# Moving two thirds of one layer's conditioning product from TensorE to row sums on VectorE

## What is computed

```python
for l in range(2):
    mod  = silu(c)     @ w_ada[l] + b_ada[l]      # 6 x 1024 numbers, for x
    cmod = silu(c_ctx) @ w_ada[l] + b_ada[l]      # 6 x 1024 numbers, for xc
    shift1, scale1, gate1, shift2, scale2, gate2 = split(mod, 6)
    y, yc = mixer(x * (1 + scale1) + shift1, xc * (1 + cscale1) + cshift1)   # GLA, MLA and conv branch
    x = layer_norm(ALPHA * x + gate1 * y)
    x = layer_norm(ALPHA * x + gate2 * conv_ffn(x * (1 + scale2) + shift2))
    # the same for xc with cmod, in layer 0 only
```

## Time and profile before

| | us |
|---|---|
| median of 3 runs | 2666.77 (2665.58 to 2667.77) |
| the profiled execution | 2666.24 |
| its span | 2664.2 |
| PE busy | 2612.0, 98% |
| DVE busy | 1852.5, 70% |
| ACT busy | 827.1, 31% |
| GpSimd (POOL) busy | 87.1, 3% |

### The profile page before, as it was taken

How to read it: one execution, slowest core, us unless ns; L and a number is a source line. 1 busy time by engine, 2 the same in 40 slices (tenths; PEclk the granted TensorE clock), 3 DMA queues, 4 the chain that set the end, 5 groups by cost and what they waited for, 6 DMA issues and landing times.

```text
span 2664.2 us, 43805 instructions
## 1 busy us (share of the span) xinstructions
PE 2612.0 (98%) x17212; PEld 2213.2 (83%) x17212; DVE 1852.5 (70%) x3779; ACT 827.1 (31%) x1856; POOL 87.1 (3%) x115
## 2 busy tenths in 40 slices
PE   9999899999999999999999999999999999999998
PEld 8777799979676887567887888888799987898998
DVE  7882299644787377788857766644467568768997
ACT  2033144132554112553232423200445222133431
POOL 0000000000231000000000000000012000000000
PEclk9999999999999999999999999999999999999999
DMA  5553544432332221221222222222321431243443
GB/s 209 183 191 119 215 159 160 178 126 85 118 140 88 80 95 72 87 95 72 81 94 95 95 79 95 80 95 95 116 73 58 149 135 64 95 150 136 163 171 127
DMA packets 86922, 314.21 MB, mean 118 GB/s; under 512 B 9488, under 2 KB 11536, under 8 KB 86464
## 3 DMA queue, kind: packets, MB, share of 16 engines
q1 hardware_dynamic: 85216, 304.78, 32.1%
q0 software_dynamic: 1504, 6.64, 0.7%
HBM read 310.33 MB, written 1.05 MB: 117 GB/s over the span
## 4 chain that ended last, share of the span: by engine, by line
PE 68%; DVE 3%; ACT 1%; issue 1%; DMA 0%; DVEq 0%; ACTq 0%; SPq 0%
PE ps L621 39%; PE ps L924 14%; PE ps L730 2%; PE ps L3460 1%; PE ps L3377 1%; PE ps L3378 1%; PE ps L3325 1%; PE ps L937 1%; PE ps L3429 1%; PE ps L962 1%; PE ps L1815 1%; PE ps L2130 1%; PE ps L2294 1%; PE ps L2248 0%; PE ps L2271 0%
## 5 line engine op out<-in xcount | busy, mean ns | idle before, releaser
L621 PE MATMUL ps<-sb 128*128 128x128 f32 (+1 forms) x8344 | 1353.7, 325 | 7.2 <-ACT sb L697 3.3
L621 PEld LDWEIGHTS ps<-sb 128*128 128x128 f32 x8344 | 1244.7, 191 | 118.2 <-issue 8.5
L924 PE MATMUL ps<-sb 128*128 128x256 f32 (+1 forms) x2320 | 612.3, 421 | 8.8 <-DVE sb L1003 3.7
L924 PEld LDWEIGHTS ps<-sb 128*128 128x128 f32 x2320 | 439.0, 190 | 167.8 <-issue 101.3
L3638 DVE SCALAR_TENSOR_TENSOR sb<-sb 128x512 f32<-128x512 f32 (+1 forms) x480 | 275.5, 615 | 8.7
L793 ACT COPY sb<-ps 128x256 f32<-128x256 f32 (+1 forms) x221 | 76.4, 346 | 406.0 <-PE ps L621 342.5
L634 DVE TENSOR_TENSOR sb<-sb 128x512 f32<-128x512 f32 x160 | 109.7, 686 | 128.0 <-PE ps L621 90.9
L697 ACT COPY sb<-ps 128x128 f32<-128x128 f32 (+1 forms) x252 | 75.3, 299 | 217.9 <-PE ps L621 211.7
L811 DVE TENSOR_TENSOR sb<-sb,ps 128x256 f32<-128x256 f32 (+1 forms) x118 | 45.5, 386 | 103.0 <-PE ps L621 73.1
L636 DVE TENSOR_TENSOR sb<-sb 128x512 f32<-128x512 f32 x160 | 110.6, 692 | 5.5
L4282 DVE SCALAR_TENSOR_TENSOR sb<-sb 128x512 f32<-128x512 f32 (+1 forms) x176 | 101.0, 615 | 14.6 <-ACT sb L4228 9.6
(11 more groups left out here) (533 smaller groups left out, 2749.7 us busy)
## 6 DMA issues: line engine op xcount, KB each, us to landing
sb<-in_w SPq DMA_DIRECT2D x575, 512.0 KB, 3.7
sb<-in_two POOLq DMA_DIRECT2D x2, 1088.0 KB, 7.3
sb<-in_x SPq DMA_DIRECT2D x2, 512.0 KB, 4.8
sb<-in_ctx POOLq DMA_DIRECT2D x1, 1024.0 KB, 7.8
sb<-in_v_bias POOLq DMA_DIRECT2D x2, 512.0 KB, 3.6
sb<-in_par SPq DMA_DIRECT2D x1, 764.0 KB, 6.6
sb<-in_s5b POOLq DMA_DIRECT2D x1, 512.0 KB, 7.8
sb<-in_s5c POOLq DMA_DIRECT2D x1, 512.0 KB, 9.8
```

The costliest lines, as they stand in the source:

```text
L621: ins = pe.matmul(o, w, xs(i), start=(fresh and i == 0), stop=(i == len(ws) - 1), skip_group_check=True)
L924: ins = pe.matmul(o[:, i * n:(i + 1) * n], w, rhs(k), start=(k == 0), stop=(k == kt - 1))
```

## The change

Layer 1's groups 0 to 7 (blocks a = 0 to 31) are taken from PE. Groups 8 to 11 stay, at the places that are left: two before the first GLA unit, one in head 3, one in the closing of the layer norm. The 32 blocks come from a transposed copy of the weights, `wa`: 32 tiles of 128 outputs x 1024 inputs, 512 KB each. `crow` holds c and c_ctx, each repeated on 128 partitions (512 KB each). ACT applies silu to `crow` in place. DVE multiplies a tile by a silu'd row and sums along it in one scalar_tensor_tensor with `accum_out`. Blocks 16 to 31 are wanted for x alone (one such instruction each) and are computed in `v_gla_in(0)`; blocks 0 to 15 are wanted for x and context (two each) and are computed in the down projection of layer 0's FFN. So 48 instructions of 128x1024 are added. `wa` and `crow` come by GpSimd's queue into 3 buffers in the first place and 4 in the second; a buffer is filled again when DVE is done with the block in it. The coefficients of layer 1's first modulation (`v_coef(1, 0)`) and two scalings move from the start of `v_ln_close` to the end of the last turn of the down projection.

```diff
-ADA_HEADS = (1, 3, 5)
+ADA_HEADS = (3,)
+ADA_COLUMNS = list(range(16, 32)) + list(range(16))
+ADA_EARLY = 16
+ADA_BY_PE = [list(range(6 * D // 512)), list(range(8, 6 * D // 512))]
+ROW_BUFS = (3, 4)
...
-        ADA_FILL = {"start": 2, 1: 1, 2: 1, 3: 1, 4: 1, 5: 1, 6: 1}
+        ADA_FILL = {"start": 2}
...
+        def p_columns(e):
+
+            first = e * ADA_EARLY
+            for i in range(first, ADA_EARLY if e == 0 else len(ADA_COLUMNS)):
+                _, b, _ = column_buf(i)
+                if i - first >= ROW_BUFS[e]:
+                    po.wait_ge(vector_steps, at(("column", i - ROW_BUFS[e])))
+                po.dma_start(column_bufs[e][:, b, :], t_in["wa"][i]).then_inc(column_loaded[b], 16)
+
+        def p_cond_rows(e):
+            for c in range(1 + e):
+                po.dma_start(cond_rows[e][:, c, :], t_in["crow"][c]).then_inc(loaded["crow%d" % e], 16)
+
+        def a_cond_rows(e):
+            act.wait_ge(loaded["crow%d" % e], at("loaded_crow%d" % e))
+            for c in range(1 + e):
+                act.activation(cond_rows[e][:, c, :], cond_rows[e][:, c, :], ACT.Silu).then_inc(scalar_steps, A.step(("crow", e)))
...
+        def v_columns(n):
+            for i in range(column_next[0], column_next[0] + n):
+                e, b, turn = column_buf(i)
+                a, w = ADA_COLUMNS[i], column_bufs[e][:, b, :]
+                ve.wait_ge(scalar_steps, at(("crow", e)))
+                ve.wait_ge(column_loaded[b], 16 * (turn + 1))
+                if e:
+                    if i > ADA_EARLY:
+                        ve.wait_ge(vector_steps, at(("product", i - 1)))
+                    ve.scalar_tensor_tensor(out=product_out, in0=w, scalar=1.0, in1=cond_rows[e][:, 1, :], op0=ALU.mult, op1=ALU.mult,
+                                            accum_out=mod[:, 1, a, 1:2]).then_inc(vector_steps, V.step(("product", i)))
+                    ve.wait_ge(vector_steps, at(("product", i)))
+                ve.scalar_tensor_tensor(out=w, in0=w, scalar=1.0, in1=cond_rows[e][:, 0, :], op0=ALU.mult, op1=ALU.mult,
+                                        accum_out=mod[:, 1, a, 0:1]).then_inc(vector_steps, V.step(("column", i)))
+            column_next[0] += n
...
@@ a_gla_in, behind the two reads of k
+            if l == 0:
+                a_cond_rows(0)
             key, b = ("kp", l, 2), [pc(("b_in", l, "k"), m) for m in (2, 3)]
@@ v_gla_in
             v_pair_parts(g, ("kp", l, 2), lambda m, c: kT[:, 2 + m, c * TX:(c + 1) * TX])
+            if l == 0:
+                v_columns(3)
...
                     pair_sums(g, i)
+                    v_columns(3)
                     key = ("qp", l, m)
...
                 pair_sums(g, i + 1 + j)
+                if l == 0:
+                    v_columns((1, 2, 2, 2)[j])
+                    if j == 3:
+                        v_columns_bias(16, 32, 1)
@@ v_down_parts, turn p
+            by_columns = f.tag == ("f2", 0)
+            if by_columns and p in (1, 2):
+                v_columns(2)
             for q in (3 * p + 2, 3 * p + 3):
                 if q < 12:
                     down_sums(f, q)
+                if by_columns and q == 3 * p + 2:
+                    v_columns(3)
+            if by_columns and p == 3:
+                v_columns_bias(0, 16, 2)
+                f.columns_done()
@@ a_r
+            if (l, m) == (0, 0):
+                act.wait_ge(vector_steps, at(("column", ADA_EARLY - 1)))
@@ gpsimd
                 po.dma_start(two, t_in["two"]).then_inc(loaded["two%d" % l], 16)
                 if l == 0:
+                    p_cond_rows(0)
+                    p_columns(0)
                     for u, unit_ in enumerate(units(l)):
                         p_gla_prod(l, u, *unit_)
...
                 p_pads(l)
+                if l == 0:
+                    po.wait_ge(vector_steps, at(("u2", 0, FT - 1)))
+                    p_cond_rows(1)
+                    p_columns(1)
```

More of the change, by code:

```diff
@@ L264, in build @@
         slab_loaded = [sem(f"slab_loaded{i}") for i in range(RING)]
-        loaded = {n: sem("loaded_" + n) for n in ("x0", "x1", "par", "one", "rows1", "s5", "two0", "two1", "rowsl0", "rowsl1", "cond", "ctx")}
+        loaded = {n: sem("loaded_" + n) for n in ("x0", "x1", "par", "one", "rows1", "s5", "two0", "two1", "rowsl0", "rowsl1", "cond", "ctx", "crow0", "crow1")}
+        column_loaded = [sem(f"column_loaded{i}") for i in range(4)]
         out_stored = sem("out_stored")
@@ L1809, in t_ada @@
                 pe.wait_ge(scalar_steps, at("cond"))
-            o = open_job(("ada", l), hold=True) if j == 0 else ps[:, job_of[("ada", l)], :]
+            first = j == ADA_BY_PE[l][0]
+            o = open_job(("ada", l), hold=True) if first else ps[:, job_of[("ada", l)], :]
             c0 = 2 * (ADA - 1 - j)
@@ L1814, in t_ada @@
                 q = 32 * (k % 4)
-                ins = pe.matmul(o[q:q + 32, :], cond[:, k, c0:c0 + 32], w, start=(j == 0 and k < 4), stop=(j == ADA - 1 and k >= 4),
+                ins = pe.matmul(o[q:q + 32, :], cond[:, k, c0:c0 + 32], w, start=(first and k < 4), stop=(j == ADA - 1 and k >= 4),
                                 skip_group_check=True)
@@ L1822, in more_ada @@
             for _ in range(n):
-                t_ada(ada_done[0] // ADA, ada_done[0] % ADA)
+                l, j = [(l, j) for l in range(LAYERS) for j in ADA_BY_PE[l]][ada_done[0]]
+                t_ada(l, j)
                 ada_done[0] += 1
@@ L1847, in v_ada_tr, with column_buf @@
                                  ALU.add).then_inc(vector_steps, V.step(("free", ("adt", l))))
             ve.wait_ge(vector_steps, V.n)
-            for part in range(2):
+            for part in range(l, 2):
                 a0 = (3 * part + 1) * DT
                 ve.tensor_scalar(mod[:, l, a0:a0 + DT, :], mod[:, l, a0:a0 + DT, :], 1.0, None, ALU.add).then_inc(vector_steps, V.step(("mod", l)))
+        def column_buf(i):
+            e = int(i >= ADA_EARLY)
+            q = i - e * ADA_EARLY
+            b = q % ROW_BUFS[e]
+            return e, b, q // ROW_BUFS[e] + (len(range(b, ADA_EARLY, ROW_BUFS[0])) if e and b < ROW_BUFS[0] else 0)
@@ L3920, in v_coef @@
         def v_coef(l, part, gain, beta):
+            w = 1 if (l, part) == (1, 1) else 2
             a = coef[:, 2 * l + part]
[L3923 to L3926, removed]
+            up = mod[:, l, (3 * part + 1) * DT:(3 * part + 2) * DT, 0:w]
+            by = lambda key: pc(key, 0, DT).unsqueeze(2).to_broadcast([P, DT, w])
             ve.wait_ge(vector_steps, V.n)
-            ve.tensor_tensor(a[:, DT:2 * DT, :], a[:, DT:2 * DT, :], mod[:, l, 3 * part * DT:(3 * part + 1) * DT, :], ALU.add).then_inc(vector_steps, V.step(("coef", l, part)))
+            ve.tensor_tensor(a[:, 0:DT, 0:w], up, by(gain), ALU.mult).then_inc(vector_steps, V.step())
+            ve.tensor_tensor(a[:, DT:2 * DT, 0:w], up, by(beta), ALU.mult).then_inc(vector_steps, V.step())
+            ve.wait_ge(vector_steps, V.n)
+            ve.tensor_tensor(a[:, DT:2 * DT, 0:w], a[:, DT:2 * DT, 0:w], mod[:, l, 3 * part * DT:(3 * part + 1) * DT, 0:w], ALU.add).then_inc(vector_steps, V.step(("coef", l, part)))
         def part_of(gate):
@@ L3939, in v_ln_close, with next_coef @@
                 v_turns(mix_src[l])
-            if nxt is not None:
+            def next_coef():
                 v_coef(*nxt, gain, beta)
@@ L4292, in build @@
         for n_, s_ in loaded.items():
[L4293 removed]
+            known_val = {"s5": 32, "rowsl0": 32, "rowsl1": 32, "cond": 16, "crow1": 32}.get(n_, 16)
             table["loaded_" + n_] = (n_, known_val)
@@ L4596, in _layout @@
     return m
-_SHAPES = dict(x=(P, DT, TX), ctx=(P, DT, TX), cond=(P, CONDW * DT), one=(P, len(ONE_NAMES), P), two=(P, TWO_COLS), par=(P, len(PARAMS)),
+_SHAPES = dict(wa=(len(ADA_COLUMNS), P, D), crow=(2, P, D), x=(P, DT, TX), ctx=(P, DT, TX), cond=(P, CONDW * DT), one=(P, len(ONE_NAMES), P), two=(P, TWO_COLS), par=(P, len(PARAMS)),
                rows1=(P, ROWS_1), s5b=(P, 2 * S5_TILES * 32), s5c=(P, 2 * S5_TILES * 32), rowsl=(LAYERS, P, 512), v_bias=(LAYERS, P, 1024))
```

29 lines of the change are left out of this document (25 added, 4 removed).

## The result

The changed kernel takes 2654.52 us (median of 4 runs, 2651.56 to 2655.41) against 2667.27 (4 runs, 2665.58 to 2670.03): ratio 0.9949, 95% interval 0.9932 to 0.9966. The direction and most of the mechanism held; the size did not.

The account below looks back on a forecast made before the run. PE was taken as the bound, busy 2612.0 of 2664.2 us. Removed groups -12.1 and ACT's delay +3.7, with sums and queues at nothing, gave -8.4 on the median 2666.77: 2658.4 us, range 2654 to 2664.

Parts of the forecast that it names:

- What is removed: Eight 1.92 us groups off PE in GLA units 1 to 6 and MLA heads 1 and 5: 12.1 us gained.
- What ACT gets: Start of input projections: table load and silu delay ACT's copy of P1; PE idles 2.0 us, 3.7 with clock loss.
- The clock term: Behind PE's 2.0 us idle stretch in the input projections, 3.3 us at half clock lose 1.7 us.
- the row lands early or the clock stays: Rival, input projections: cost 0.4 in place of 3.7 us, 2655.1 us; clock alone kept, 2656.7; chance 0.18.
- DVE's sums: 48 sums of 1.23 us in input projections and down projection, hidden in DVE's waits: cost nothing.
- the first early place: Start of the input projections: DVE was said to wait about 4.5 us for PE, covering three sums of 3.7 us.
- The rival of half rate: Accumulating sums take 2.46 us; some 2 us reach the path at the last late place: 2660.4 us, chance 0.10.
- The slower rival: Columns' round trip, refill 8.7 us, leaves DVE standing and PE stalling in the projections: 2674 us, chance 0.08.
- the last place: Tightest late place, end of the down projection: six sums end by 1856.7, P1 read at 1859.45, hidden by 2.7 us.

Follow-up runs that it names:

- e11: Changed kernel with each late column's context sum made three times (32 more sums in the down projection): 2680.04 us, ratio to before 1.0043.
- e10: Changed kernel with each early column summed twice (16 more sums on DVE): 2653.99 us, ratio to before 0.9955.
- e13: Changed kernel with three columns (1.5 MB) issued by GpSimd ahead of the conditioning row: 2662.81 us, ratio to before 0.9982.
- e6: Changed kernel with the silu behind the copies of P1 and head 3's group moved to GLA unit 2: 2653.04 us, ratio to before 0.9946.
- e2: Changed kernel with the first column (512 KB) issued by GpSimd ahead of the conditioning row: 2655.39 us, ratio to before 0.9960.
- e4: Changed kernel without the added sums, rows and columns, groups still removed (the table's second column; result not the reference's): 2654.14 us, ratio to before 0.9953.
- e9: Changed kernel with two buffers in place of three for the early columns: 2655.84 us, ratio to before 0.9956.

## Why the prediction missed in size

- **What is removed**, forecast 12.1, measured 13.1 (neither). Place by place, from the second column of the table: start and unit 1 2.46 (forecast 1.92), unit 2 and unit 3 together 2.07 (0 + 1.92), unit 4 2.05, unit 5 2.06 (1.92 each), unit 6 0.81 (0.6), the heads 3.83 (3.84), with 0.17 given back between. Which units give and which don't was read rightly from the earlier trace rows. The surplus of the first place is not the group's: before, the clock is at half behind the wait of 1.27 us for weights there, and in the other trace it isn't, though its wait is 0.6 longer.
- **What ACT gets** is the step that failed: 2.0 us of waiting and 1.7 of clock, where the changed kernel shows a wait of 0.50 and full clock. The first goes back to "it lands 8.7 us later, 560.85" for `two`. In the changed kernel the DMA rows of the same stretch (us from issue to landing at the end) are

```profile
sb<-in_two POOLq DMA_DIRECT2D x1, 1088.0 KB, 7.5
...
sb<-in_crow POOLq DMA_DIRECT2D x1, 512.0 KB, 8.2
```

  GpSimd issues them at 554.81 and 555.33: landings at 562.3 and 563.5, the row 1.2 behind `two`, against my 1.4 for its 512 KB. That part held. But `two` took 7.5 us, and in the fourteen traces, in which its issue and all ahead of it are the same, it took 6.3 to 8.7, 7.9 in the middle. The 8.7 of the earlier trace rows is the longest of them. One execution's transfer time was used as if it were the kernel's. PE's wait follows it, in the kernels that leave the row and the silu where they are: 0.30 us with 6.3 and 7.1 (there the table load ends last), 0.50 with 7.5, about 0.95 with 7.9, 1.27 with 8.2. Carried on to 8.7 that is an estimated 1.7, near my 2.0. I did give bounds, 0.4 to 4.3, but put the value at a row that has no spread beside it.
- **The clock term**, 1.7 us, was added to the unhappy value and is not borne out even for it: a wait of 2.58 us at the same place, made on purpose, was followed by full clock in its one trace. Together the two terms were forecast at 3.7 us and measured at 0.75 in the projections and 0.57 in the end. That is 3.1 of the miss, the removed work the other 1.0; -8.4 less both is -12.5, what the changed kernel's trace shows. That is the rival "the row lands early or the clock stays", -11.7 us, to which I gave 0.18: by its two costs, though not by its reason, for the row did not pass `two`.
- **DVE's sums** were priced rightly (1.22) and hidden in all 13 places; PE waits for DVE in none of them. One reading was off without harm: the 4.5 us of the first early place is a wait for a weight's DMA (4.56 in the timeline), not for PE. The Trainium skill's rule that I weighed, half rate for a scalar_tensor_tensor with two SBUF sources that aren't bf16 ("Vector Engine (DVE) Microarchitecture Reference", "Points that are easy to get wrong"), doesn't show here with an accumulator either: 128x1024 fp32 in 1.22 us.
- **The rival of half rate** had a wrong price, 2 us. e11, which adds as many late sums and by their dependence a little more time, cost 21.7; 32 times 1.15 alone is 36.8 against 23.4 left, 13 us without any loss of clock. The early half costs nothing (e10). I looked at the last place alone; the six waits that I listed for the stage make 55.0 us in all (9.47, 7.64, 9.82, 6.99, 9.46, 11.66 in the timeline of the kernel before), and sums at half rate would need 73.6. I should have made that sum.
- **The slower rival**, the columns' round trip, is real, but starts only below two buffers: with one the gain is gone, with two nothing is lost. My price of 8.7 us for a refill took one issue's worst case for the rule; the median of the early ones was 5.5.

Left open: what decides whether the clock falls behind a wait of 1 to 3 us, and why the first block's length differs by up to 7.5 us from execution to execution. Neither was tried by itself. Both only blur the comparisons here, by 1 to 2 us a time.

## What to carry to other kernels

Work taken off the engine that sets the pace is worth its length at each place where the next one is not waiting for someone else, and the place tells you: the same group of matmuls was worth 2.05 to 2.07 us in three units, 1.9 in each of two heads, 0.8 in one unit and nothing in another, where it could stay for free. For what is put in its place, sum the hiding engine's idle time over the whole stage as well as at the tightest point, since a deficit is handed on and comes out where the reserve ends. And the landing of one transfer in one trace is a draw: a term that hangs on it wants the spread of such landings, and no second term should be built on it.

## What the runs showed of the hardware

- Waits of PE and the granted clock behind them: 0.50 followed waits of 1.27 and 1.93 us (before), 1.63 (e10), 1.67 and 7.05 (e13), 1.85 (e6) and 1.96 (e2); full clock followed 1.94 (the changed kernel, at the very place of before's 1.93), 1.34, 1.48, 1.58, 1.86 (e4 and e9, at the very place of e6's 1.85), 2.12 in unit 2, and 2.58. Here is the changed kernel's, to be held against the earlier trace rows:

```profile
2420.53 0.70 PE L3961 MATMUL ps<-sb 128*128 128x256 f32 x2 [1.94 <-DVE sb L4177]
...
2421.00:2422.00 1.00, 0.91 (x5) 0.63 (x4) 0.27 (x1) 0.98 (x2) 0.00 (x0) 1.00 1.02 410
```

  The length of the last idle stretch alone doesn't tell. A clock term for a single wait of some 2 us is a coin, not a price.
- A scalar_tensor_tensor with `accum_out` shows as two rows, 1.22 us and a DVE_READ_ACCUMULATOR of 0.08 that the next one overlaps: 1.15 us from one sum to the next for 128x1024 fp32, 1.26 where the next waits for it (e11).
- `two`, 1088 KB on GpSimd's queue from the same place of the program with the same transfers ahead of it, took 6.3 to 8.7 us from issue to landing over fourteen executions. A single trace gives such a time to within a microsecond or so only.
- GpSimd's queue moved 25 MB beside the ring's 287 MB over the whole execution, and PE's waits for the ring's weights between 558 and 1900 us were 2.5 us in all, against 1.9 before; in the projections a 512 KB column landed in 5.5 us (median) with three in flight.
